# One core, encoder block with expert-choice routing: the second half's top-128 search on two lists of 320, places looked up, two first low parts on VectorE

## The reference

```
cap = CAPACITY_FACTOR * n_tok // N_EXPERTS
aff = jax.nn.softmax((t @ w_router).astype(jnp.float32), axis=-1)
gates, idx = lax.top_k(aff.T, cap)
xs = t[idx]
hid = jax.nn.silu(jnp.einsum('ecd,edf->ecf', xs, w_gate)) * jnp.einsum('ecd,edf->ecf', xs, w_up)
out = jnp.einsum('ecf,efd->ecd', hid, w_down) * gates[..., None].astype(t.dtype)
y = jnp.zeros_like(t).at[idx.reshape(-1)].add(out.reshape(-1, D))
```

## Time and profile before

| | |
|---|---|
| median of three timed executions | 2149.66 us (2145.63 to 2150.45) |
| the profiled execution's own time | 2150.63 us |
| its span, first to last instruction | 2148.8 us |
| PE busy | 2099.9 us, 98% |
| DVE busy | 1221.5 us, 57% |
| ACT busy | 940.4 us, 44% |
| POOL busy | 674.4 us, 31% |
| mean granted TensorE clock | 0.990 of full |

### The profile page before, as it was taken

One profiled execution on the slowest core, in us unless ns is written; L12 is line 12 of the kernel. 1 busy time (PEld: TensorE's weight loads), 2 busy tenths in 40 slices (PEclk: granted clock), 3 DMA queues, 4 the chain that ended last, 5 costly groups with the idle time before them and its releaser, 6 DMA issues.

```text
span 2148.8 us, 33481 instructions
## 1 busy us (share of the span) xinstructions
PE 2099.9 (98%) x13406; PEld 1729.2 (80%) x13406; DVE 1221.5 (57%) x1431; ACT 940.4 (44%) x1180; POOL 674.4 (31%) x431
## 2 busy tenths in 40 slices
PE   8999999999999999999999999699999999999997
PEld 8888888888888888888888888577777777777775
DVE  5344601222375567777655338866766666676764
ACT  5112311211455366666641032365556565555653
POOL 2333221212355366666643500221112211112111
PEclk9999999999999999999999999799999999999999
DMA  5122224544676642223134432588878888877883
GB/s 174 59 88 86 72 94 127 165 132 145 209 265 232 212 142 84 67 67 111 40 110 141 173 113 108 206 315 317 305 271 305 291 307 300 301 295 281 301 291 97
DMA packets 184230, 397.41 MB, mean 185 GB/s; under 512 B 15696, under 2 KB 103760, under 8 KB 184144
## 3 DMA queue, kind: packets, MB, share of 16 engines
q1 hardware_dynamic: 169552, 343.78, 44.6%
q0 software_dynamic: 7680, 20.98, 4.0%
q10 hardware_dynamic: 6912, 31.46, 3.7%
HBM read 317.53 MB, written 78.64 MB: 184 GB/s over the span
## 4 chain that ended last, share of the span: by engine, by line
PE 89%; DVE 5%; ACT 2%; DMA 2%; issue 1%; POOL 0%; SPq 0%; ACTq 0%; DVEq 0%; POOLq 0%
PE PS L1416 25%; PE PS L370 14%; PE PS L372 14%; PE PS L371 14%; PE PS L1447 8%; PE PS L1230 2%; DVE small L2147 1%; PE PS L1217 1%; PE PS L1221 1%; PE PS L1218 1%; PE PS L1219 1%; PE PS L1220 1%; PE PS L1163 1%; ACT prob L1782 1%; PE PS L1122 1%
## 5 line engine op out<-in xcount | busy, mean ns | idle before, releaser
L370 PE MATMUL PS<-act_hi,w_hi 128*128 128x512 f32 (+1 forms) x1072 | 383.4, 358 | 0.0
L372 PE MATMUL PS<-act_hi,w_lo 128*128 128x512 f32 (+1 forms) x1072 | 376.0, 351 | 0.0
L371 PE MATMUL PS<-act_lo,w_hi 128*128 128x512 f32 (+1 forms) x1072 | 375.8, 351 | 0.0
L872 POOL TENSOR_SCALAR prob<-prob,small 128x1024 f32<-128x1024 f32 (+1 forms) x80 | 200.6, 2508 | 120.6 <-DVE small L2162 120.6
L372 PEld LDWEIGHTS PS<-act_hi,w_lo 128*128 128x128 f32 x1072 | 202.8, 189 | 27.5
L370 PEld LDWEIGHTS PS<-act_hi,w_hi 128*128 128x128 f32 x1072 | 203.1, 189 | 26.4 <-DVE act_lo L2037 0.7
L371 PEld LDWEIGHTS PS<-act_lo,w_hi 128*128 128x128 f32 x1072 | 203.3, 190 | 25.5 <-issue 0.7
L775 POOL TENSOR_SCALAR w_hi<-w_raw 128x1024 fp32r<-128x1024 f32 x46 | 49.5, 1076 | 420.9 <-PE PS L372 393.8
L1416 PE MATMUL PS<-ehi,xT_hi 128*128 128x512 f32 x520 | 167.7, 404 | 0.2 <-DVE elo L2365 0.2
L1416 PE MATMUL PS<-elo,xT_hi 128*128 128x512 f32 x520 | 160.8, 390 | 0.0
L1416 PE MATMUL PS<-ehi,xT_lo 128*128 128x512 f32 x520 | 160.5, 390 | 0.0
(11 more groups left out here) (339 smaller groups left out, 4816.0 us busy)
## 6 DMA issues: line engine op xcount, KB each, us to landing
raw<-in_w_gate SPq DMA_DIRECT2D x64, 1024.0 KB, 10.4
raw_more<-in_w_up SPq DMA_DIRECT2D x32, 1024.0 KB, 6.7
raw_w<-in_w_up SPq DMA_DIRECT2D x32, 1024.0 KB, 10.8
w_raw<-in_w_in SPq DMA_DIRECT2D x35, 512.0 KB, 4.0
w_raw<-in_w_down SPq DMA_DIRECT2D x15, 1024.0 KB, 4.9
stg<-in_w_down SPq DMA_DIRECT2D x15, 1024.0 KB, 6.9
gt<-in_w_down SPq DMA_DIRECT2D x15, 1024.0 KB, 11.3
raw_end<-in_w_down SPq DMA_DIRECT2D x15, 1024.0 KB
```

What stands on the lines that cost most here:

```text
L370: pe.matmul(out, lh, rh, start=first, stop=False)
L371: pe.matmul(out, lh, rl, start=False, stop=False)
L372: return pe.matmul(out, ll, rh, start=False, stop=last)
L872: pool.tensor_scalar(prob[:, n % 3, 0:kn], prob[:, n % 3, 0:kn], prec[:, s:s + 1], None, ALU.mult).then_inc(S["norm_pool"], 1)
```

## The change

**The list.** Instead of the second half's 512 affinities on 16 partitions, group 1 searches 640 values: the first half's 128 chosen (`tops[0]`, already in falling order) and the second half's 512. They lie on 32 partitions: partitions 0 to 15 hold the 128 chosen, chunk 4 and half of chunk 5, partitions 16 to 31 the other half of chunk 5 and chunks 6 and 7, so each is 320 wide (`WIDE`). `turn_pairs` builds that bank with six float32 matrix products in place of four transposes; `pairs` is the softmax with zeros on both sides, so that a product can put it on either half of the partitions.

**The merge.** The two lists of 128 that come out are merged as before, but the reversal is a copy with falling addresses on VectorE (`turned_up`), and all four pieces are transposed by one step (`turn_both`). The waits for `chosen_act` and the `flip` product go.

**The places.** A place under 128 in the first list is not a token but a place in `tops[0]`. For each expert `spread_tokens` broadcasts the row `shift` (token less 384 less place) to all partitions with a float32 product, 4 experts inside the last `out_product`, 12 after the last logits; ScalarE copies the four banks (`table_copy`) into `hid` and `ob_p`, and VectorE looks up (`look_up`): one operation over 128 columns an expert that keeps the value whose column equals the place, and a sum. Expert 0 is looked up at once for `ixg_p`, the other 15 in `frame(0)` ahead of piece 3's `elo`.

**Low parts.** `first_low(1)` leaves GpSimd; VectorE makes the low parts of pieces 1 and 2 ahead of group 2's search, and `first_rows_lo(0)` moves into the search, behind 8 of its 11 operations.

```diff
-                work = sb(s2, "work", [E, HALF])
+                work = sb(s2, "work", [2 * E, HALF])
+                pairs = sb(s2, "pairs", [P, HC, 3 * E])
...
+        WIDE = (HALF + P) // 2
+        TOKEN_C = HALF - P
...
+                if isinstance(e, int) and e == 1:
+                    pool.wait_ge(S["rows_dve"], ROWS_P)
...
-            for q in range(2):
-                first_low(q)
+            first_low(0)
...
+            def turn_pairs():
+                out = PS[0:2 * E, BANK:BANK + WIDE]
+                pe.wait_ge(S["r_dve"], 10)
+                pe.matmul(out[:, 0:P], ident[0:E, 0:2 * E], tops[0][:], start=True, stop=False)
+                pe.matmul(out[:, P:2 * P], pairs[:, 0, E:3 * E], ident[:], start=False, stop=False)
+                pe.matmul(out[:, 2 * P:WIDE], pairs[:, 1, E:3 * E], ident[:, 0:P // 2], start=False, stop=False)
+                pe.matmul(out[:, 0:P // 2], pairs[:, 1, 0:2 * E], ident[:, P // 2:P], start=False, stop=False)
+                pe.matmul(out[:, P // 2:P // 2 + P], pairs[:, 2, 0:2 * E], ident[:], start=False, stop=False)
+                pe.matmul(out[:, P // 2 + P:WIDE], pairs[:, 3, 0:2 * E], ident[:], start=False, stop=True).then_inc(S["aff_pe"], 1)
...
+            def turn_both(b):
+                pe.wait_ge(S["topk_dve"], TOPK[1])
+                for n, src in enumerate((tops[1][:], topf[1][:], turned_up[:, 0], turned_up[:, 1])):
+                    last = pe.transpose(bank(b)[:, 2 * n * E:2 * (n + 1) * E], src, ident[0:2 * E, 0:2 * E])
+                last.then_inc(S["chosen_pe"], 1)
+
+            def spread_tokens(e0, en):
+                for e in range(e0, e0 + en):
+                    last = pe.matmul(bank((1, 2, 3, 5)[e // 4])[:, e % 4 * P:(e % 4 + 1) * P], ident[0:E, e:e + 1].to_broadcast([E, P]),
+                                     shift[:], start=True, stop=True)
+                last.then_inc(S["chosen_pe"], 1)
...
-                        turn_lists(1)
+                        turn_pairs()
+                    if k == 3 and (c, h) == (NCH - 1, 0):
+                        pe.wait_ge(S["affT_act"], 2)
+                        spread_tokens(0, 4)
...
-            turn_chosen(0, 2)
-            pe.wait_ge(S["chosen_act"], 1)
-            pe.matmul(bank(3)[:, 0:2 * E], flip[:], chosen[:].rearrange("p v e -> p (v e)"), start=True,
-                      stop=True).then_inc(S["chosen_pe"], 1)
-            turn_chosen(1, 4)
+            spread_tokens(4, E - 4)
+            turn_both(4)
+            pe.wait_ge(S["chosen_act"], 4)
             turn_lists(2)
...
-            select(1, 0, 8)
+            select(1, 0, 11)
             second_norm(8)
-            select(1, 8, 26)
+            select(1, 11, 35)
             second_norm(9)
-            select(1, 26, PICKS)
+            select(1, 35, PICKS)
             numbers(1)
+            kstep(dve.tensor_copy(turned_up[:, 0], tops[1][:, ::-1]))
+            kstep(dve.tensor_copy(turned_up[:, 1], topi[1][:, ::-1]))
...
+            def look_up(e):
+                t = (hid, ob_p)[e // 8][:, e % 8 * P:(e % 8 + 1) * P]
+                return dve.scalar_tensor_tensor(out=t, in0=counted[:], scalar=code[:, e:e + 1], in1=t, op0=ALU.is_equal,
+                                                op1=ALU.mult)
...
+                        dve.wait_ge(S["chosen_act"], 4)
+                        for x in range(1, E):
+                            last = look_up(x)
```

More of the change, by code:

```diff
@@ L2279, in _ @@
                 residual(c, 0)
+            kstep(dve.memset(pairs[:], 0.0))
             for c in range(HC):
@@ L2325, in _ @@
                                      op1=ALU.subtract).then_inc(S["rows_dve"], 1)
-            dve.wait_ge(S["rows_dve"], 2)
-            chosen_step(dve.tensor_tensor(pick[:, 2], pick[:, 0], pick[:, 1], ALU.mult), 3)
-            dve.scalar_tensor_tensor(out=ixg_p[:], in0=pick[:, 2, 0:1], scalar=float(HALF), in1=ib[:, 0:1], op0=ALU.add,
+            dve.wait_ge(S["rows_dve"], 3)
+            chosen_step(dve.tensor_tensor(pick[:, 2], pick[:, 0], pick[:, 1], ALU.mult), 4)
+            chosen_step(dve.scalar_tensor_tensor(out=code, in0=pick[:, 2], scalar=float(WIDE), in1=ib, op0=ALU.add,
+                                                 op1=ALU.add), ROWS_C)
@@ new lines, in _ @@
+            dve.wait_ge(S["chosen_act"], 1)
+            def look_up(e):
+                t = (hid, ob_p)[e // 8][:, e % 8 * P:(e % 8 + 1) * P]
+                return dve.scalar_tensor_tensor(out=t, in0=counted[:], scalar=code[:, e:e + 1], in1=t, op0=ALU.is_equal,
+                                                op1=ALU.mult)
+            chosen_step(look_up(0), ROWS_C + 1)
+            chosen_step(dve.tensor_reduce(found[:, 0:1], hid[:, 0:P], AX_X, ALU.add), ROWS_C + 2)
+            dve.scalar_tensor_tensor(out=ixg_p[:], in0=code[:, 0:1], scalar=float(TOKEN_C), in1=found[:, 0:1], op0=ALU.add,
@@ L2329, in _ @@
                                      op1=ALU.add).then_inc(S["ix_g"], 1)
-            chosen_step(dve.scalar_tensor_tensor(out=rows[:, 0], in0=pick[:, 2], scalar=float(HALF), in1=ib, op0=ALU.add,
-                                                 op1=ALU.add), ROWS_P)
             dve.tensor_tensor(gates[:, 0], va, vb, ALU.max)
             def first_rows_lo(h):
-                dve.wait_ge(S["xh_act" if h else "chosen_act"], 1 if h else 3)
+                dve.wait_ge(S["xh_act" if h else "chosen_act"], 1 if h else 5)
@@ L2340, in _ @@
             affinities(2)
-            dve.wait_ge(S["e_hi"], 3)
-            dve.tensor_tensor(elo[:, 2], raws[2], f32(ehi[:, 2]), ALU.subtract).then_inc(S["e_lo"], 1)
-            select(2, 0, PICKS_S)
+            for q in (1, 2):
+                dve.wait_ge(S["e_hi"], q + 1)
+                dve.tensor_tensor(elo[:, q], raws[q], f32(ehi[:, q]), ALU.subtract).then_inc(S["e_lo"], 1)
+            select(2, 0, 8)
             first_rows_lo(0)
+            select(2, 8, PICKS_S)
             for top in (tops[2], topi[2]):
@@ L2367, in frame @@
                         first_rows_lo(1)
+                        dve.wait_ge(S["chosen_act"], 4)
+                        for x in range(1, E):
+                            last = look_up(x)
+                        chosen_step(last, ROWS_S + 1)
+                        dve.tensor_reduce(found[:, 1:8], hid[:, P:].rearrange("p (e j) -> p e j", j=P), AX_X, ALU.add)
+                        chosen_step(dve.tensor_reduce(found[:, 8:E], ob_p[:].rearrange("p (e j) -> p e j", j=P), AX_X, ALU.add),
+                                    ROWS_S + 2)
+                        chosen_step(dve.scalar_tensor_tensor(out=rows[:, 0], in0=code, scalar=float(TOKEN_C), in1=found[:],
+                                                             op0=ALU.add, op1=ALU.add), ROWS_P)
                     if is0 and n == 5:
```

97 lines of the change are left out of this document (58 added, 39 removed).

## The result

The changed kernel takes 2158.29 us (median of five executions, 2155.03 to 2159.61), the kernel before 2149.66 in the same comparison: a ratio of 1.0040, 95% interval 1.0025 to 1.0055. It is slower. The prediction said 2153.4 with a range up to 2158.0; the direction and the place of the loss were right, its size was not.

What follows compares the result with a forecast made beforehand. PE bounds the kernel, except before G, where the searching engine decides, then the gather's latency. Gain at G -3.6, stall +5.0, clock +2.3 sum to +3.7 us: 2153.4 against the median 2149.66, range 2147.6 to 2158.

Steps and rivals of the forecast that it cites:

- The gain at G: G is the end of `ixg_p`, ahead of expert 0's gather; the shorter search brings it 3.6 us earlier, bounds 2.2 to 5.0.
- nothing is changed in the gather: Behind G: the gather stays as before (7.51 us), so expert 0's first product stays at G + 9.8.
- the stall: In frame 0, PE waits 5.0 us at piece 3 for VectorE's `elo`, late behind look-ups and sums.
- the low clock behind it: PE's clock falls after the wait at piece 3 and costs 2.3 us, ends 0 and 2.9.
- Search round: VectorE's search in group 1: a round takes 1.68 us at 320 columns, against 2.28 at 512.
- The look-ups: On VectorE ahead of piece 3's `elo`: fifteen at 0.27 us each, 4.0; with sums, rows and gaps 6.7.
- The added PE work in the stream: Ahead of the last residual: `turn_pairs` 0.6 us later, four spreads in the last `out_product` 0.86; together 1.5.
- The twelve spreads: On PE after the last logits: 3.9 us, the middle of 2.6 at 2.4 GHz and 5.2 at 1.2 GHz; they end last.
- VectorE was forecast ready: After the search, cast and two copies, ahead of the turn of the lists: at 1370.5, against 1377.6 before.
- the third rival: SyncE's four loads go out about one us ahead of the gather, not six: gather +1.9 us, 2155.3; chance 0.12.
- low clock at the first product: Rival: PE idles some 3.3 us before the gather lands, expert 0's first product takes 6 us: +3.0, 2156.4; chance 0.25.
- Not slower: Rival: no stall at piece 3, look-ups and sums fit the 1.4 us slack: 2146.1; chance 0.13 including smaller gains.

Runs made afterwards that it cites:

- the filled stall: Changed kernel with 40 more PE transposes ahead of piece 3, into a bank nobody reads: 2153.97 us, 1.0025 to the kernel before.
- two low parts on GpSimd: Changed kernel with GpSimd making the first low parts of pieces 0 and 1, VectorE piece 2 only: 2159.60 us, 1.0052 to the kernel before.
- turn ahead of the spreads: Changed kernel with `turn_both` issued before the twelve spreads, not behind them: 2158.28 us, 1.0048 to the kernel before.
- second changed profile: The changed kernel, no edit, profiled once more: median 2156.63 us, 1.0040 to the kernel before; the profiled execution took 2155.49.
- first mix: Changed kernel with look-ups spread over pieces 3, 5 and 7, `turn_both` before the spreads, GpSimd's low part after VectorE's copies: 2150.00 us, 1.0005 to the kernel before.

## Why the prediction was wrong in size

Two steps of the prediction failed. The gain at G was forecast as 3.6 us and was 1.5, and "nothing is changed in the gather, so the first product stays at G + 9.8" did not hold: it came at G + 11.1. Of the 3.6 us only 0.2 was left at the first product, while the stall and the low clock behind it came nearly as forecast.

**Search round, place of the stall, its size: right.** A round took 1.68. The look-ups took 0.26 each (forecast 0.27), the sums 1.0 and 1.2 in the stream (1.1 and 1.25), the stall was 4.63 (5.0), and the clock behind it cost 2.15 in the profile and 2.7 by the filled stall (2.3).

**The gain at G: the term that failed.** It was forecast as 3.6 with bounds of 2.2 to 5.0. From the turn, G came 1.46 earlier (41.54 to 40.08), or 0.59 with the last transposes at half clock. Three sizes make that up. The added PE work in the stream cost 2.27, not 1.5: the turn 0.9 more than before, not 0.6, and the rest, 1.4, with the four spreads, not 0.86. The sum had counted columns alone. The twelve spreads ran at 1.2 GHz to the end, 5.28 instead of 3.9: the prediction had taken the middle because the clock might rise on the way, and PEclk stayed 0.50 from 1364 to 1372.2. And in eight of the twelve profiles the last transposes, too, ran at half clock (0.87). VectorE was forecast ready 12.2 us behind the last residual (1370.5 against 1358.3); without GpSimd's hold it would have been at 12.1, with it it was at 14.4, still ahead of the spreads, which end at 15.8.

**The gather: "nothing is changed in the gather" was wrong.** It took 8.8 instead of 7.5, and the first product came at G + 11.1, not G + 9.8. This was the third rival, given 0.12. That loads in flight make the gather later is shown by the run that puts them behind it. That their new place, 2.2 us ahead and not 5.9, is what made 8.8 out of 7.5 is not: with two low parts on GpSimd they stood 5.8 ahead, and the gather took 8.6; with the turn ahead of the spreads they stood 1.8 ahead, and it took 8.0. With the slower gather the first product starts 51.16 behind the turn against 51.35: **all but 0.2 us of the gain is used up by then**.

**The sum.** Forecast: -3.6 + 5.0 + 2.3 = +3.7. By the profiles: -0.2 + 4.63 + 2.15 = +6.6. Of the 3.4 that the first term lacks, 2.1 are G's and 1.3 the gather's. The end of piece 3 is 69.6 against 62.8 and 63.0, and behind it all take nearly the same time to the end of the span (changed 749.0 and 748.9, before 748.6 and 748.7). The medians say +8.6 in one group and +7.6 in the other. The second changed profile has 0.87 of the difference; a low clock at the first product, 1.5 us in the edited kernels' profiles that show it, could give the rest, and the mean clock of the slower executions would fit, but no such execution of the changed kernel was profiled. That part stays open.

**Rivals.** "Not slower" fell: the 6.3 us of look-ups were there. The low clock at the first product was seen in four profiles of edited kernels and in neither of the changed kernel. That GpSimd's low part holds VectorE's small operations was not among the rivals; it cost nothing here by luck, since the spreads ended later still, and 3 us where that luck was taken away.

## What to carry to other kernels

When work is moved off the path, ask which list it lands in and how much slack stands in front of the next due operation there: fifteen operations of 0.26 us and two sums cost 6 us (2156.63 against 2150.65 without them) in front of a buffer that was 1.4 us early, and nothing clear of the intervals when spread over three places. Of a step made shorter, price what its neighbours do in the time freed: the loads that are in flight beside a gather, the engine whose long operation holds the small ones. A gain ahead of a later bound should be counted only up to that bound: with the loads behind the gather the first product came 2.9 us earlier, and the ratio hardly moved.

## What the runs showed of the hardware

- A copy or cast from SBUF to SBUF on VectorE of 0.21 us took 2.56, 3.44 or 4.42, and a two-input one of 0.18 took 3.27 or 0.92, each until a 4.5 us subtraction of GpSimd ended. Beside it MAX8, FIND_INDEX8 and MATCH_REPLACE8 (0.48, 0.47, 0.46), operations with an input from PSUM (0.17) and ScalarE's copies (0.29) were not held.
- The same gather of 128 rows took 4.6 us with SyncE's four loads issued behind it, 7.5 and 7.6 in the kernel before with them 5.9 us ahead, and 8.0 to 9.9 with them in flight in the kernels with the change. How far ahead they stand doesn't order these: at 5.8 us it took 8.6 (two low parts on GpSimd), at 1.8 us 8.0 (turn ahead of the spreads) and 9.9 (first mix). Why is open.
- MAX8 took 0.41 over 256 columns on 16 partitions, 0.48 over 320 on 32 and 0.68 over 512 on 16: some 1.04 ns a column, whatever the partitions, as forecast.
